# Dual layers: three and a half tiles of the first gate product are multiplied inside the attention loop into a bank of their own; attention outputs use one bank

## The chip, the cores and the metric

One core of a Trainium2 chip runs the whole program in one launch. The metric is device microseconds from the start to the end of an execution. All inputs and outputs are float32.

## The reference, cut to what matters

Two models run one behind the other on 256 tokens of width 1024. The change lies in the second, whose two layers are called "dual" here. Each layer has three branches (a convolution, a neighbourhood attention with 8 heads, a grouped-query attention with 8 query and 2 key heads) and a gate for each branch:

```python
a, naq, nak, nav, gq, gk, gv, gates = split_in(h @ w_in[l])
br_a = conv_branch(a, ...)                                  # layer norm over 512 channels, silu, @ w_conv_out
br_b = na_latent(naq, nak, nav, na_kc, na_vc, na_rpb[l]) @ w_na_out[l]
q = axial_rope(rmsnorm_2(gq, q_norm_g[l]), pos_row, pos_col)
k = axial_rope(rmsnorm_2(gk, k_norm_g[l]), pos_row, pos_col)
br_c = gqa_latent(q, k, gv, g_kc, g_vc) @ w_gqa_out[l]
ga, gb, gc = jnp.split(gates, 3, axis=-1)                   # 3 x 1024 columns of h @ w_in[l]
y = jax.nn.sigmoid(ga) * br_a + jax.nn.sigmoid(gb) * br_b + jax.nn.sigmoid(gc) * br_c
x = x + g1 * (y @ w_out[l])
```

In layer 0 the 256 context tokens go through the same layer beside the 256 latent ones (512 columns, N = 512); in layer 1 only the latent ones do (N = 256), and the context gives keys and values. `g1` and its like come from `silu(c) @ w_mod + b_mod`.

## The kernel before

**Products.** Each weight product is made of three products of rounded parts (`product`, line 698: high by high, high by low, low by high), accumulated in a PSUM bank. A tile of an output is 128 rows by N columns; with an inner dimension of 1024 it has 8 "k steps" of three products each. A "job" is 8 weight tiles of 128 by 128, enough for one output tile of a gate. Weights come as halves of 16 tiles (1 MB) into a ring of four slots, through SP's queue, in the order of STREAM. ACT rounds a job (`round_job`), DVE subtracts to get the low part (`rest_job`, line 1613), and PE waits for that. Four split jobs have room; `ahead(stage, g)` on ACT and on DVE handles the job three behind g. So when the attention loop begins, jobs 0 to 2 of the first gate product are split, and `ahead("gates..", 0)` is the call that splits job 3, `ahead(.., 1)` that of job 4.

**The attention loop** (`softmax`, one version for each of PE, ACT and DVE). A step v takes a pair of heads. PE: the scores of pair v (`score_pair`, banks 4 to 7), at even v the output product of pairs v - 4 and v - 3, then the turns (transposes) of pair v - 2 into banks 2 and 3. DVE: the bias of the neighbourhood heads, the maximum, later the scaling by the inverse sum. ACT: a copy of the turned probabilities, the exponentials, and at odd v, behind the exponentials, the copy of the outputs (`o_free`). Layer 0 has 32 pairs (16 grouped-query, 16 neighbourhood; 2 of each 4 against all 512 keys, 2 against 256), layer 1 has 16. The outputs lie by turns in banks 0 and 1 (`out_banks`), so PE waits for the output copy of two before.

**What follows.** PE waits for the last output copy and multiplies the gate tiles in two groups of four (`gemm_group`, banks 0 to 3). After the fourth and the eighth tile it makes two sums of the convolution's layer norm (`conv_sums`), for which POOL adds the four chunks (`add_chunks`, line 639; `ln_added`); the second of these additions needs ACT's squares of the centred values, which need the first sum. ACT takes the sigmoid of each tile. Then come the 8 tiles of `branch{l}0`, 4 k steps each, and the same for the other two gates.

In layer 0, DVE also has the dot products for the modulation of later layers (`dots`, `mod_half`, line 1634; eight instructions each) behind the splits of tiles 1, 2, 3 and 6, with their weights in the same ring. They need Silu of c: POOL loads c when all outputs are copied (line 633), and ACT takes the Silu behind the sigmoid of tile 0, ahead of everything for tile 1.

Of the kernel before, what the change touches and what calls it, by code (L numbers as in the profile page):

```python
# [45 lines left out]
DH = 64  # L46
# [109 lines left out]
for _name in DOTS_AT:  # L156
# [7 lines left out]


BANKS = [("lru_in", (5,) * 4), ("lru_gate", (0, 0, 0, 0, 3, 3, 2, 2)), ("lru_out", (1,) * 8),
         ("ffn_in0", (12,) * 4), ("ffn_out0", (2,) * 4), ("nsa_q", (2,) * 4), ("nsa_kv", (2,) * 4),
         ("nsa_gate", (0, 0, 1, 0)), ("nsa_v", (1, 1, 0, 0)), ("gate_turned", (0, 0, 0, 1)), ("cmp", (2, 2, 0, 0)),
         ("cmp2", (0, 0, 0, 0, 0, 0, 1, 1)), ("nsa_out", (2,) * 4), ("ffn_in1", (12,) * 4), ("ffn_out1", (2,) * 4)]
for _l in range(DEPTH):  # L170
    BANKS += [(f"conv_in{_l}", (2,) * 4), (f"gq{_l}", (1,) * 4), (f"gkv{_l}", (1, 0, 1, 1)),
              (f"naq{_l}", (1,) * 4), (f"nak{_l}", (1,) * 4), (f"nav{_l}", (1, 1, 0, 0, 0, 0, 1, 1))]
    for _b in range(3):
        BANKS += [(f"gates{_l}{_b}", (2,) * 4), (f"branch{_l}{_b}", (2,) * 4)]
    BANKS += [(f"out{_l}", (2,) * 4), (f"mlp_in{_l}a", (HALF_A,) * 4), (f"mlp_out{_l}a", (2,) * 4),
              (f"mlp_in{_l}b", (HALF_B,) * 4), (f"mlp_out{_l}b", (2,) * 4)]
# [118 lines left out]
def program(nc, wstream, params_in, consts_in, rpb_in, c_in, x_in, out):  # L295
    ctx = ExitStack()
    with ctx:
# [3 lines left out]
        def sem(name):  # L301
            return ctx.enter_context(nc.semaphore(name))
# [123 lines left out]
        cmp_scores = [ps[q][:, 0:HEADS * NCMP] for q in range(2)]  # L426
        nav_banks = (0, 1, 6, 7)

        landed = [sem(f"landed{s}") for s in range(SLOTS)]
# [31 lines left out]
        rotated, centred = sem("rotated"), sem("centred")  # L461
        ln_added = sem("ln_added")
        blocks_ready = sem("blocks_ready")
        branch_rounded, branch_split = sem("branch_rounded"), sem("branch_split")
# [193 lines left out]
        def _(pe):  # L658
# [201 lines left out]

            def softmax(layer=None, begun=0, after={}):

# [3 lines left out]
                for v in range(pairs + 3):  # L866
                    if begun <= v < pairs:
                        score_pair(layer, v)
                    if v >= 4 and v % 2 == 0:

                        i = 2 * (v - 4)
                        kind, t, _, q = jobs[i]
                        out_ = (base + i) // 4
                        if out_ >= 2:
                            pe.wait_ge(o_free, out_ - 1)
                        if layer is None and i == 0:
                            pe.wait_ge(pe_aux_free, 2)
                        if layer is not None and i < 8:
                            pe.wait_ge(acc_free[out_ % 2], USED[f"nav{layer}"][out_ % 2] + 1)
                        pe.wait_ge(turned_ready, (base + i) // 2 + 2)  # L880
# [18 lines left out]
                        for n in range(last + 1):  # L899
                            for p in range(2):  # L900
                                val, pr, first = terms[p][n]
                                ins = mm(out_banks[out_ % 2][DH * p:DH * p + DH, first * P:S], val, pr, start=n == 0, stop=n == last)
                        ins.then_inc(o_full, 1)
# [147 lines left out]
            def dual(l):  # L1051
# [85 lines left out]
                turned_group(f"nav{l}", nav_banks, (f"in{l}", 22), 512, after=in_nav)  # L1137
                softmax(l, begun=2)
                pe.wait_ge(o_free, jobs_done.base // 4)
# [14 lines left out]
                for br in range(3):  # L1154
                    for n in range(2):
                        gemm_group(f"gates{l}{br}", f"gates{l}{br}", n, n, N=N, between=conv_sums(n) if br == 0 else None)
# [29 lines left out]
        def _(act):  # L1186
# [162 lines left out]
            def softmax(layer, after):  # L1349

                jobs = attention_jobs(layer)
                pairs = len(jobs) // 2
                base = jobs_done.base
                for v in range(pairs + 4):
                    if 2 <= v < pairs + 2:
# [6 lines left out]
                        if kind == "nsa" and u == 0:  # L1362
                            act.wait_ge(c_copied, 2)
                        go(used_pair(pT[:, (2 * u) % 4:(2 * u) % 4 + 2, :], kind, q), used_pair(turn_pair, kind, q), ACT.Copy).then_inc(turned_ready, 1)
                    if v < pairs:
                        kind, t, _, q = jobs[2 * v]
                        act.wait_ge(score_max, base // 2 + v + 1)
                        for p in range(2):
# [6 lines left out]
                            ins.then_inc(prob_exp, 1)  # L1375
                    if v >= 5 and v % 2 == 1:
                        n = 2 * (v - 5)
                        kind, t, _, q = jobs[n]
                        out_ = (base + n) // 4
                        act.wait_ge(o_full, out_ + 1)  # L1380
                        o = {"nsa": n_q, "na": a_naq, "gqa": a_gq}[kind]
                        go(o[:, t, q * P:(q + 2) * P], out_banks[out_ % 2][:, 0:S], ACT.Copy).then_inc(o_free, 1)
                    if v in after:
# [54 lines left out]
            def dual(l):  # L1438
# [51 lines left out]

                softmax(l, {1: nav_copies})

                def branch_round(br):

                    if br == 0:
                        act.wait_ge(o_free, jobs_done.base // 4)
                    else:
                        full(f"branch{l}{br - 1}", 3, 1)
# [5 lines left out]
                for br in range(3):  # L1504
                    for n in range(2):
                        for m in range(4):
                            ahead(f"gates{l}{br}", 4 * n + m)
                            copy(f"gates{l}{br}", m, n, a_sig[:, 4 * n + m, 0:N], acc[m][:, 0:N], func=ACT.Sigmoid)
                            if (l, br, n, m) == (0, 0, 0, 0):
# [52 lines left out]
        def _(dve):  # L1562
# [451 lines left out]
            def dual(l):  # L2014
# [103 lines left out]
                dve.wait_ge(conv_done, KC * (l + 1))  # L2118
                softmax(l)

                for br in range(3):
                    st = f"branch{l}{br}"
                    for g in range(8):
                        ahead(f"gates{l}{br}", g)

                        if (br, g) == (0, 4):
                            dve.wait_ge(pe_aux_full, aux.next())
                            link(V.tensor_scalar(rs[:, 0:N], psT[:, 0:N], 1.0 / CW, None, ALU.mult))
                            for c in range(KC):
                                V.tensor_tensor(a_cy[:, c, 0:N], a_cy[:, c, 0:N], rs[:, 0:N], ALU.subtract).then_inc(centred, 1)  # L2130
# [12 lines left out]
                    for m in range(KD + 2 * (br == 2)):  # L2143
# [7 lines left out]
                        if m < 4:  # L2151
                            dve.wait_ge(acc_free[m], USED[f"gates{l}{br}"][m] + 2)
                        o, g, a = a_y[:, m, 0:N], a_sig[:, m, 0:N], acc[m % 4][:, 0:N]
# [222 lines left out]
```

## Time and profile before

| | |
|---|---|
| three runs | 2074.39, 2073.84, 2060.24 us |
| median | 2073.84 us |
| the profiled execution | 2069.44 us, span 2067.6 us |
| mean granted clock of TensorE | 0.982 |
| instructions | 33690 |

Times in rows are microseconds from the span's start. PE is TensorE's products, PEld its weight loads, DVE VectorE, ACT ScalarE, POOL GpSimd. A row of the timeline gives start, duration, engine, line, operation, output<-inputs by name with the shape, the count of merged instructions, and in brackets the idle time ahead with what ended it. Ends of matmuls are modelled, so that neighbouring ones overlap in the rows: the distance from start to start is the cost of one. L666 is a helper that makes all products, L1198 one that makes all ACT operations; their tiles tell which is meant.

### The profile page before, as it was taken

To read this page: it belongs to the slowest core of one execution; us is meant where nothing else is said; L and a number is where in the kernel's file an instruction comes from. 1 tells how busy PE (TensorE), PEld (TensorE's weight loads), DVE (VectorE), ACT (ScalarE), POOL (GpSimd) and SP (SyncE) were. 2 spreads that over 40 slices of the span, in tenths; PEclk is the share of its full clock that TensorE was granted. 3 is DMA by queue.
4 is the path that set the end of the run, shared out by engine and by line. 5 is a ranking of instruction groups with operands and counts; after the bars stand their busy time and mean duration, and the time that the engine had idled before them with its cause. 6 is when DMAs were issued, how large, how long until landed. Compare 5 with 4: busy or idle time off the path is not lost.

```text
span 2067.6 us, 33690 instructions
## 1 busy us (share of the span) xinstructions
PE 1984.2 (96%) x12854; PEld 1748.1 (85%) x12854; DVE 1506.5 (73%) x2738; ACT 897.0 (43%) x1436; POOL 361.4 (17%) x354
## 2 busy tenths in 40 slices
PE   7999999979999999988999999999999998999998
PEld 6999999759999888646888878888888866999998
DVE  7769887697987589776697668575666986675554
ACT  5744445463444432476333332222214456644442
POOL 0013333002325300001100222201231000013223
PEclk9999999999999999999999999999999999999999
DMA  6455575405555422102445225454554311554552
GB/s 259 165 198 190 198 258 191 176 8 218 202 184 207 149 102 83 61 1 97 149 163 194 102 81 201 148 201 184 185 210 164 130 55 42 181 187 164 185 201 82
DMA packets 46990, 318.12 MB, mean 154 GB/s; under 512 B 5008, under 2 KB 8080, under 8 KB 9488
## 3 DMA queue, kind: packets, MB, share of 16 engines
q1 hardware_dynamic: 45568, 309.58, 41.3%
q0 software_dynamic: 1296, 6.82, 1.0%
q8 instruction: 84, 1.38, 0.3%
q14 instruction: 42, 0.34, 0.0%
HBM read 315.33 MB, written 1.05 MB: 153 GB/s over the span
## 4 chain that ended last, share of the span: by engine, by line
PE 86%; DVE 8%; ACT 4%; issue 1%; DMA 0%; POOL 0%; DVEq 0%; ACTq 0%; POOLq 0%
PE ps L666 84%; ACT arena L1198 3%; PE ps L915 2%; DVE arena L2037 2%; DVE small L1843 1%; DVE w_lo L1613 1%; DVE arena L1865 1%; DVE ps L1832 1%; ACT w_hi L1198 1%; DVE arena L1595 0%; ACT L1198 0%; DMA x<-x_in 0%; PE ps L1104 0%; PE ps L1097 0%; DVE rs L1794 0%
## 5 line engine op out<-in xcount | busy, mean ns | idle before, releaser
L666 PE MATMUL ps<-h_hi,w_hi 128*128 128x256 f32 (+2 forms) x2632 | 838.1, 318 | 21.5 <-DVE h_lo L1605 8.2
L666 PE MATMUL ps<-h_lo,w_hi 128*128 128x256 f32 (+2 forms) x2632 | 830.2, 315 | 0.0
L666 PE MATMUL ps<-h_hi,w_lo 128*128 128x256 f32 (+2 forms) x2632 | 829.7, 315 | 0.0
L1613 DVE TENSOR_TENSOR w_lo<-ring,w_hi 128x1024 fp32r<-128x1024 f32 x457 | 583.9, 1284 | 300.0 <-ACT w_hi L1198 299.2
L1198 ACT ACTIVATE w_hi<-ring 128x1024 fp32r<-128x1024 f32 x457 | 479.5, 1055 | 527.3 <-PE ps L666 491.7
L666 PEld LDWEIGHTS ps<-h_hi,w_hi 128*128 128x128 f32 (+1 forms) x2632 | 499.2, 190 | 60.6 <-issue 14.3
L666 PEld LDWEIGHTS ps<-h_lo,w_hi 128*128 128x128 f32 (+1 forms) x2632 | 500.9, 190 | 33.4
L666 PEld LDWEIGHTS ps<-h_hi,w_lo 128*128 128x128 f32 (+1 forms) x2632 | 499.2, 190 | 33.5
L1198 ACT ACTIVATE arena<-ps 128x512 f32<-128x512 f32 (+2 forms) x246 | 140.8, 578 | 343.1 <-PE ps L666 296.3
L666 PE MATMUL ps<-hid_hi,w_hi 128*128 128x256 f32 (+1 forms) x736 | 224.2, 305 | 0.0
L666 PE MATMUL ps<-hid_lo,w_hi 128*128 128x256 f32 (+1 forms) x736 | 224.2, 305 | 0.0
L666 PE MATMUL ps<-hid_hi,w_lo 128*128 128x256 f32 (+1 forms) x736 | 224.1, 305 | 0.0
L1634 DVE SCALAR_TENSOR_TENSOR ps<-ring,arena 128x512 f32<-128x512 f32 x320 | 223.6, 766 | 0.0
L555 POOL CAST hid_hi<-arena 128x256 f32 (+3 forms) x92 | 45.5, 495 | 576.8 <-DVE arena L1778 576.8
L666 PEld LDWEIGHTS ps<-hid_lo,w_hi 128*128 128x128 f32 x736 | 139.0, 189 | 6.8
L666 PEld LDWEIGHTS ps<-hid_hi,w_lo 128*128 128x128 f32 x736 | 138.2, 188 | 6.9
L666 PEld LDWEIGHTS ps<-hid_hi,w_hi 128*128 128x128 f32 x736 | 138.2, 188 | 6.8
L557 POOL TENSOR_TENSOR hid_lo<-arena,hid_hi 128x256 f32 (+3 forms) x92 | 138.8, 1509 | 15.1 <-POOL hid_hi L555 14.4
L666 PE MATMUL ps<-arena 128*64 128x256 f32 (+4 forms) x768 | 124.4, 444 | 17.4 <-ACT arena L1198 15.0
L2037 DVE SCALAR_TENSOR_TENSOR arena<-arena,prm 128x512 f32<-128x512 f32 (+1 forms) x240 | 129.7, 608 | 0.0
L562 POOL TENSOR_TENSOR arena<-x 128x256 f32<-128x256 f32 (+1 forms) x59 | 58.8, 996 | 294.1 <-DVE x L1995 219.0
L666 PEld LDWEIGHTS ps<-arena 128*64 128x64 f32 (+2 forms) x768 | 59.2, 160 | 57.3 <-issue 35.8
(193 smaller groups left out, 1944.4 us busy)
## 6 DMA issues: line engine op xcount, KB each, us to landing
ring<-wstream SPq DMA_DIRECT2D x290, 1024.0 KB, 4.8
arena<-c_in POOLq DMA_DIRECT2D x7, 512.0 KB, 4.1
arena<-rpb POOLq DMA_DIRECT2D x2, 1536.0 KB, 6.5
x<-x_in SPq DMA_DIRECT2D x2, 1024.0 KB, 12.0
out<-arena SPq DMA_DIRECT2D x8, 128.0 KB, 2.0
cst<-consts SPq DMA_DIRECT2D x1, 928.0 KB, 12.0
prm<-params SPq DMA_DIRECT2D x1, 580.0 KB, 10.7
ring<-wstream SPq DMA_DIRECT2D x1, 512.0 KB, 3.8
```

The lines of the kernel that those rows point to most:

```text
L555: nc.gpsimd.tensor_copy(hi, products[:, e, 0:N]).then_inc(pool_step, 1)
L557: nc.gpsimd.tensor_tensor(lo, products[:, e, 0:N], hi.bitcast(F32), ALU.subtract).then_inc(pool_written, 1)
L562: square = nc.gpsimd.tensor_tensor(total if first else one, src, src, ALU.mult)
L666: ins = nc.tensor.matmul(*a, **k)
L915: ins = nc.tensor.transpose(turn_pair[:, p, b * P:(b + 1) * P], s_p[:, (2 * u + p) % 4, b * P:(b + 1) * P], ident)
L1198: return nc.scalar.activation(o, i, f, **k)
L1613: V.tensor_tensor(w_lo[:, job % SPLITS, :], raw_job(job), w_hi[:, job % SPLITS, :].bitcast(F32), ALU.subtract).then_inc(weights_ready, 1)
L1634: V.scalar_tensor_tensor(out=ps[4 + p][:], in0=w, scalar=1.0, in1=c[s][:, p * S2:(p + 1) * S2], op0=ALU.mult, op1=ALU.mult, accum_out=mod_ ...
L1832: ins = V.scalar_tensor_tensor(out=sc, in0=c, scalar=slope, in1=sc, op0=ALU.mult, op1=ALU.add)
L1843: ins = V.tensor_reduce(top, used_pair(score_pairs[v % 2], kind, q), AX, ALU.max, negate=True)
L1865: ins = V.tensor_scalar(o[:, br, :], o[:, br, :], s_rec[:, c:c + 1], None, ALU.mult)
L2037: return V.scalar_tensor_tensor(out=cy[:, c, 0:ns, :], in0=a_u3[:, c, 0:ns, bass.ds(j, S)], scalar=w, in1=cy[:, c, 0:ns, :], op0=ALU.mult, ...
```

## The change

Of the first gate (`gates{l}0`) tiles 0, 1 and 2 and the first four k steps of tile 3 move into PE's attention loop. In layer 0 one k step stands in each of v 3 to 10, 12 to 19 and 21 to 28, and four in v 34, the last; in layer 1 two stand in each of v 3 to 6, 8 to 11 and 13 to 16, and four in v 18, the last. A step stands behind the scores and ahead of the output product. Tiles 0 to 2 go one after another into bank 1. The outputs have bank 0 alone, so that PE waits for the output copy of one before, and ACT makes this copy ahead of the exponentials of the odd v. ACT copies each finished tile to SBUF in the loop (places that are free by then) and takes the three sigmoids from there after the loop. The split of job 3 moves into the loop as well (ACT v 16 and 8, DVE v 18 and 9). The second half of tile 3 stands ahead of the wait for the last output copy; tiles 4 to 7 follow, with the sums after tiles 4 and 7.

```diff
+FILL = 3
+FILL_AT = {0: [(v, 1) for first in (3, 12, 21) for v in range(first, first + KD)] + [(34, 4)],
+           1: [(v, 2) for first in (3, 8, 13) for v in range(first, first + KD // 2)] + [(18, 4)]}
+FILL_DONE = {0: (10, 19, 28), 1: (6, 11, 16)}
+FILL_USES = (1, 4, 1, 2)
+def gate_bank(br, m):
+    if br == 0:
+        return (1, m) if m < FILL else (m % 4, {3: 0, 4: 0, 5: FILL, 6: 0, 7: 1}[m])
+    return m % 4, m // 4
...
+        gate_raw = (rs, part(16640, S2), a_nak[:, 2, :])
+        def out_half(layer, i):
+            return out_banks[i % 2 if layer is None else 0][:, 0:S]
...
+            def gate_steps(l, N):
+                step, at = {}, 0
+                todo = [(m, k) for m in range(FILL + 1) for k in range(KD)]
+                def some(count):
+                    nonlocal at
+                    for m, k in todo[at:at + count]:
+                        b, n = gate_bank(0, m)
+                        if k == 0:
+                            step[m] = job(f"gates{l}0", m)
+                            free(f"gates{l}0", b, n)
+                        ins = product(acc[b][:, 0:N], step[m](k), h_(k, 0, N), k == 0, k == KD - 1)
+                        if k == KD - 1:
+                            ins.then_inc(acc_full[b], 1)
+                            job_done()
+                    at += count
+                return some
...
 # PE, attention loop
                     if begun <= v < pairs:
                         score_pair(layer, v)
+                    if v in amid:
+                        amid[v]()
                     if v >= 4 and v % 2 == 0:
...
-                        if out_ >= 2:
+                        if layer is not None:
+                            pe.wait_ge(o_free, out_)
+                        elif out_ >= 2:
                             pe.wait_ge(o_free, out_ - 1)
...
-                softmax(l, begun=2)
+                gates = gate_steps(l, N)
+                softmax(l, begun=2, amid={v: lambda n=n: gates(n) for v, n in FILL_AT[l]})
+                gates(KD)
                 pe.wait_ge(o_free, jobs_done.base // 4)
...
+                    for m in range(KD if br else FILL + 1, KD):
+                        b, n = gate_bank(br, m)
+                        w = job(f"gates{l}0", m)
+                        free(f"gates{l}0", b, n)
+                        for k in range(KD):
+                            ins = product(acc[b][:, 0:N], w(k), h_(k, 0, N), k == 0, k == KD - 1)
+                        ins.then_inc(acc_full[b], 1)
+                        job_done()
+                        if m in (4, 7):
+                            conv_sums(m // 7)(3)
...
 # ACT
-                softmax(l, {1: nav_copies})
+                def gate_copy(m):
+                    copy(f"gates{l}0", 1, m, gate_raw[m][:, 0:N], acc[1][:, 0:N])
+                softmax(l, {1: nav_copies, 16 // (l + 1): lambda: ahead(f"gates{l}0", 0), **{v + l: lambda m=m: gate_copy(m) for m, v in enumerate(FILL_DONE[l])}})
...
-                            ahead(f"gates{l}{br}", 4 * n + m)
-                            copy(f"gates{l}{br}", m, n, a_sig[:, 4 * n + m, 0:N], acc[m][:, 0:N], func=ACT.Sigmoid)
+                            if br + n + m:
+                                ahead(f"gates{l}{br}", 4 * n + m)
+                            if br + n + m == 0:
+                                act.wait_ge(acc_free[1], USED[f"gates{l}0"][1] + FILL)
+                                for f in (2, 0, 1):
+                                    ins = go(a_sig[:, f, 0:N], gate_raw[f][:, 0:N], ACT.Sigmoid)
+                                ins.then_inc(raw_squashed, 1)
+                            elif br or n or m >= FILL:
+                                b, turn = gate_bank(br, 4 * n + m)
+                                copy(f"gates{l}{br}", b, turn, a_sig[:, 4 * n + m, 0:N], acc[b][:, 0:N], func=ACT.Sigmoid)
                             if (l, br, n, m) == (0, 0, 0, 0):
                                 act.wait_ge(c_landed, 96)
...
 # DVE
-                softmax(l)
+                softmax(l, after={18 // (l + 1): lambda: ahead(f"gates{l}0", 0)})
```

## Rows read from the trace of the kernel before

**Rows 1.** The page's first part: busy time and share of the span.
```profile
PE 1984.2 (96%) x12854; PEld 1748.1 (85%) x12854; DVE 1506.5 (73%) x2738; ACT 897.0 (43%) x1436; POOL 361.4 (17%) x354
```

**Rows 2.** Windows of one loop period each: us, then busy time by engine, clock.
```profile
885.01:895.97 10.96, 9.69 (x68) 5.51 (x64) 7.77 (x20) 8.94 (x24) 0.00 (x0) 1.00 0.01 1
919.58:930.86 11.28, 9.75 (x64) 5.50 (x64) 8.66 (x20) 8.29 (x24) 0.00 (x0) 1.00 0.00 0
1699.16:1705.82 6.66, 6.15 (x40) 3.37 (x40) 4.77 (x11) 5.25 (x12) 0.00 (x0) 1.00 0.00 0
1705.82:1712.30 6.48, 6.15 (x40) 3.38 (x40) 5.28 (x12) 5.07 (x12) 0.00 (x0) 1.00 0.00 0
```

**Rows 3.** Timeline of layer 0's loop: waits of PE, the last at its end.
```profile
919.70 1.72 PE L666 MATMUL ps<-arena 64*128 64x256 f32 x12 [0.38 <-ACT arena L1198]
...
924.15 1.06 PE L915 MATMUL ps<-cst,arena 128*128 128x128 f32 x8 [0.57 <-ACT arena L1198]
...
953.70 1.08 PE L666 MATMUL ps<-arena 128*64 128x256 f32 x8 [0.78 <-ACT arena L1198]
```

**Rows 4.** Timeline of PE, gate products: first and last of 18, then of 19.
```profile
995.72 0.39 PE L666 MATMUL ps<-h_hi,w_hi 128*128 128x512 f32 x1
...
999.57 0.40 PE L666 MATMUL ps<-h_hi,w_lo 128*128 128x512 f32 x1
...
1763.83 0.28 PE L666 MATMUL ps<-h_hi,w_lo 128*128 128x256 f32 x1
...
1765.87 0.28 PE L666 MATMUL ps<-h_hi,w_lo 128*128 128x256 f32 x1
```

**Rows 5.** Timeline by engine from the end of layer 0's loop to the branch's end.
```profile
954.82 0.38 ACT L1198 ACTIVATE arena<-ps 128x256 f32<-128x256 f32 x1 [0.99 <-PE ps L666]
956.17 1.28 ACT L1198 ACT_TABLE_LOAD   x1
961.03 0.60 ACT L1198 ACTIVATE arena<-ps 128x512 f32<-128x512 f32 x1 [3.58 <-PE ps L666]
962.94 2.01 ACT L1198 ACTIVATE arena<-arena 128x1024 f32<-128x1024 f32 x2
964.85 1.04 ACT L1198 ACTIVATE w_hi<-ring 128x1024 fp32r<-128x1024 f32 x1
...
965.92 1.23 DVE L1613 TENSOR_TENSOR w_lo<-ring,w_hi 128x1024 fp32r<-128x1024 f32 x1 [6.96 <-ACT w_hi L1198]
...
955.50 1.04 POOL L633 DMA_DIRECT2D arena<-c_in  x2 [259.12 <-ACT arena L1198]
...
992.30 5.77 POOL L639 TENSOR_TENSOR arena<-arena 128x512 f32<-128x512 f32 x3 [30.82 <-ACT arena L1198]
...
999.80 1.03 PE L666 MATMUL ps<-arena,ones 128*128 128x256 f32 x4
1000.48 0.58 PE L666 MATMUL ps<-branch_hi,w_hi 128*128 128x512 f32 x1
...
1022.66 0.39 PE L666 MATMUL ps<-h_hi,w_hi 128*128 128x512 f32 x1
```

**Rows 6.** DMA issues of the same stretch: KB each, us to landing.
```profile
arena<-c_in POOLq DMA_DIRECT2D x2, 512.0 KB, 4.3
```

**Rows 7.** Windows around an idle stretch of PE: columns as in rows 2.
```profile
699.00:704.00 5.00, 2.73 (x10) 2.37 (x11) 2.80 (x9) 1.69 (x4) 0.00 (x0) 0.50 0.49 204
704.00:708.00 4.00, 4.00 (x11) 3.13 (x10) 4.00 (x10) 3.42 (x7) 0.00 (x0) 0.50 0.00 0
708.00:712.00 4.00, 4.00 (x18) 3.27 (x18) 4.00 (x10) 0.96 (x2) 0.00 (x0) 0.97 0.50 170
```

**Rows 8.** Timeline of layer 1: the loop's last output product, and what follows.
```profile
1739.22 3.54 PE L666 MATMUL ps<-arena 128*64 128x256 f32 x16 [1.21 <-ACT arena L1198]
...
1746.36 0.38 ACT L1198 ACTIVATE arena<-ps 128x256 f32<-128x256 f32 x1 [0.93 <-PE ps L666]
...
1759.77 3.24 POOL L639 TENSOR_TENSOR arena<-arena 128x256 f32<-128x256 f32 x3 [13.27 <-ACT arena L1198]
...
1765.99 0.61 PE L666 MATMUL ps<-arena,ones 128*128 128x128 f32 x4
```

More of the change, by code:

```diff
@@ L173 @@
     for _b in range(3):
-        BANKS += [(f"gates{_l}{_b}", (2,) * 4), (f"branch{_l}{_b}", (2,) * 4)]
+        BANKS += [(f"gates{_l}{_b}", (2,) * 4 if _b else FILL_USES), (f"branch{_l}{_b}", (2,) * 4)]
     BANKS += [(f"out{_l}", (2,) * 4), (f"mlp_in{_l}a", (HALF_A,) * 4), (f"mlp_out{_l}a", (2,) * 4),
@@ L462, in program @@
         ln_added = sem("ln_added")
+        raw_squashed = sem("raw_squashed")
         blocks_ready = sem("blocks_ready")
@@ L859, in score_pair, with softmax @@
                 ins.then_inc(score_full, 1)
-            def softmax(layer=None, begun=0, after={}):
+            def gate_steps(l, N):
[14 more added lines that the diff above has]
+                return some
+            def softmax(layer=None, begun=0, after={}, amid={}):
                 jobs = attention_jobs(layer)
@@ L877, in softmax @@
                             pe.wait_ge(pe_aux_free, 2)
-                        if layer is not None and i < 8:
-                            pe.wait_ge(acc_free[out_ % 2], USED[f"nav{layer}"][out_ % 2] + 1)
+                        if layer is not None and i == 0:
+                            pe.wait_ge(acc_free[0], USED[f"nav{layer}"][0] + 1)
                         pe.wait_ge(turned_ready, (base + i) // 2 + 2)
@@ L901, in softmax @@
                                 val, pr, first = terms[p][n]
-                                ins = mm(out_banks[out_ % 2][DH * p:DH * p + DH, first * P:S], val, pr, start=n == 0, stop=n == last)
+                                ins = mm(out_half(layer, out_)[DH * p:DH * p + DH, first * P:S], val, pr, start=n == 0, stop=n == last)
                         ins.then_inc(o_full, 1)
@@ L1154, in dual @@
                 for br in range(3):
-                    for n in range(2):
-                        gemm_group(f"gates{l}{br}", f"gates{l}{br}", n, n, N=N, between=conv_sums(n) if br == 0 else None)
+                    for n in range(2 if br else 0):
+                        gemm_group(f"gates{l}{br}", f"gates{l}{br}", n, n, N=N)
+                    for m in range(KD if br else FILL + 1, KD):
[8 more added lines that the diff above has]
+                            conv_sums(m // 7)(3)
                     for m in range(KD):
@@ L1353, in softmax, with attention_out @@
                 base = jobs_done.base
+                def attention_out(v):
+                    if v >= 5 and v % 2 == 1:
+                        n = 2 * (v - 5)
+                        kind, t, _, q = jobs[n]
+                        out_ = (base + n) // 4
+                        act.wait_ge(o_full, out_ + 1)
+                        o = {"nsa": n_q, "na": a_naq, "gqa": a_gq}[kind]
+                        go(o[:, t, q * P:(q + 2) * P], out_half(layer, out_), ACT.Copy).then_inc(o_free, 1)
                 for v in range(pairs + 4):
@@ L1364, in softmax @@
                         go(used_pair(pT[:, (2 * u) % 4:(2 * u) % 4 + 2, :], kind, q), used_pair(turn_pair, kind, q), ACT.Copy).then_inc(turned_ready, 1)
+                    if layer is not None:
+                        attention_out(v)
                     if v < pairs:
@@ L1375, in softmax @@
                             ins.then_inc(prob_exp, 1)
[L1376 to L1382, printed above, removed]
+                    if layer is None:
+                        attention_out(v)
                     if v in after:
@@ L1496, in branch_round @@
                         act.wait_ge(o_free, jobs_done.base // 4)
+                        act.wait_ge(raw_squashed, l + 1)
                     else:
@@ L2123, in dual @@
                     for g in range(8):
-                        ahead(f"gates{l}{br}", g)
+                        if br + g:
+                            ahead(f"gates{l}{br}", g)
                         if (br, g) == (0, 4):
                             dve.wait_ge(pe_aux_full, aux.next())
+                            dve.wait_ge(acc_free[3], USED[f"gates{l}0"][3] + 1)
                             link(V.tensor_scalar(rs[:, 0:N], psT[:, 0:N], 1.0 / CW, None, ALU.mult))
@@ L2151, in dual @@
                         if m < 4:
-                            dve.wait_ge(acc_free[m], USED[f"gates{l}{br}"][m] + 2)
+                            dve.wait_ge(acc_free[m], USED[f"gates{l}{br}"][m] + (2 if br else FILL_USES[m]))
                         o, g, a = a_y[:, m, 0:N], a_sig[:, m, 0:N], acc[m % 4][:, 0:N]
```

## The prediction

> **What bounds the kernel now.** I read the page first. TensorE (PE) is busy 96% of the span [rows 1], so a change that only moves products can gain no more than PE's idle time in the stretches that it touches. I looked for that next, with the busy time in windows cut at the loop's own period. In layer 0 four pairs of heads (two against 512 keys, two against 256) make a period: PE works 9.69 of 10.96 us in the grouped-query half and 9.75 of 11.28 us in the neighbourhood half, so it idles 1.27 and 1.53 us; in layer 1 two pairs make one, with 0.51 and 0.33 us idle [rows 2]. The timeline says where: each idle piece is one wait of PE on ScalarE (ACT) or VectorE (DVE), 0.4 to 0.6 us long, ahead of a score or a turn, and 0.78 us at the loop's end [rows 3]. ACT works 8.94 of 10.96 us there and DVE 7.77. The loop is a ring of three engines, with PE nearly its bound.
>
> Then I followed what starts when the loop ends in layer 0, engine by engine [rows 5]. PE goes straight on with the gate product. But another chain begins there too: the last output is copied (end at 955.2, called T0), POOL issues the load of c (955.50), ACT takes the Silu of c (962.94), rounds the next weights (964.85), DVE splits them (965.92) and works without a gap through the dot products of the modulation, which its program has between the splits; after them come the centring, the squares, POOL's additions (992.30 to 998.07) and at last the two sums on PE (999.80). In the kernel before this chain is hidden by a hair: PE reaches the second sums 1.7 us after POOL has them ready.
>
> **The change, part by part.** *Fill.* A k step of the first gate product is three products: 18 products of 512 columns start in 3.85 us (17 intervals), 0.2265 us each, so a step is 0.68 us; in layer 1, with 256 columns, 19 rows span 2.04 us, 0.113 us each, and two steps again make 0.68 us [rows 4]. 28 steps move into each layer's loop: 19.0 us of PE in layer 0, 9.5 us in layer 1. The work is the same, so the time changes only by idle time that goes or comes.
>
> *Layer 0, in the loop.* 24 single steps lie in v 3 to 28, six periods' worth. Each period gets four steps, 2.72 us, against 1.27 or 1.53 us idle, so PE becomes the bound and at most 3 x 1.27 + 3 x 1.53 = 8.4 us are absorbed [rows 2]. Are all the idle pieces reached? The 0.57 us ahead of a turn follows a score, and the step is put between; the 0.38 us ahead of a score waits for ACT's exponentials of two pairs before, and PE is now later by a step too [rows 3]. Yes, but ACT gets three copies of a finished tile (0.60 us each) and one rounding (1.05 us), DVE one split (1.23 us) inside the ring [rows 5]: together 4.1 us, with PE no longer waiting most of it is slack; I count 1.4 us. Absorbed: 7.0 us; the bounds are 8.4 and, if every step sits on the ring's latency, 0. The single bank for outputs costs nothing: an output bank is written every second v, and its 0.38 us copy is now made before the exponentials of the odd v. That copy and the moved order are covered by PE's longer round; without the cover it is 0.38 us in each of 8 periods, 3 us. The four steps at v 34 (2.72 us) stand ahead of the last output product, which waited 0.78 us [rows 3]. So the last copy, T0, is later by 19.0 - 7.0 - 0.8 = 11.2 us.
>
> *Layer 0, after the loop.* PE has only half a tile left and then tile 4. Its weights are split by the `ahead(1)` of ACT and DVE, and on ACT that stands behind the three sigmoids and the Silu of c. ACT needs 1.28 (table) + 3 x 0.60 + 1.28 = 4.4 us after T0; c lands about 0.3 + 0.5 + 4.3 = 5.2 us after T0 (issue at 955.50, the second load 0.5 later, 4.3 us each) [rows 5, 6]. The load waits for all outputs as before, so c decides: Silu at T0 + 5.2, where it was at 962.94, T0 + 7.7. The chain is therefore 2.5 us earlier against T0, and no more, while PE reaches tile 4 at T0 + 2.3. PE will wait for tile 4 until 5.2 + 2.0 (two Silu) + 1.05 + 1.23 = T0 + 9.5, and again for tiles 6 and 7 and at the second sums. From the Silu to POOL's last addition is 998.07 - 962.94 = 35.1 us of DVE, ACT and POOL, which the change leaves alone; then 0.7 us of sums and 1022.66 - 1000.48 = 22.2 us of the branch product. Before, the branch ended at T0 + 67.5; now at T0 + 5.2 + 35.1 + 0.7 + 22.2 = 63.2. Only 4.3 us of the 19.0 come back. Layer 0 so far: 11.2 - 4.3 = +6.9 us.
>
> *The clock in layer 0.* The granted clock was 1.00 nearly everywhere; where PE idled 2.3 of 5 us it was 0.50 (1.2 GHz), and in the following 4 us of full work still 0.50 and back at 0.97 in the next 4 [rows 7]: some 6 us of work at half speed, 3 us lost. PE's first new wait (T0 + 2.3 to 9.5) costs nothing so, since the chain is later anyway. The last one, from the end of tile 7 (about T0 + 36) to the sums at T0 + 40.3, is 4 us, with the branch product right behind: +3 us. Layer 0: +9.9 us. The Trainium skill (TensorE: Matmul & The Clock Gate, Part 1) says that the default state is throttled and that activity releases the throttle; the trace agrees (0.50 behind the idle stretch). By that rule alone the steps in the loop could also save: they could keep the clock up.
>
> *Layer 1.* Six times two v have steps, against 0.51 or 0.33 us idle (mean 0.42, 2.5 us), v 16 a little more, 2.8 us, less 0.7 us for the copies and the split: 2.1 us [rows 2]. The four steps at v 18 (1.36 us) fill a wait of 1.21 us. The output product behind it took 3.54 us for 16 products, at half clock, where 8 take 1.08 us in layer 0 [rows 3, 8]; with three waits of 1.2 us filled in part I expect full clock: 1.4 us saved. T0 of this layer is later by 9.5 - 2.1 - 1.2 - 1.4 = 4.8 us. Behind it there is no c: `ahead(1)` is through at 1.28 + 3 x 0.38 + 1.05 + 1.23 = 4.7 us, and PE, done with tile 3 at about 0.9, waits 3.8 us. Then four tiles of 2.72 us and 1.0 us of sums end at 16.6, where they ended at 22.8 before (from 1739.2 + 3.5 + a copy of 0.4 to 1765.99): 6.2 back, net -1.4 us. POOL's additions (to 1763.0) move forward with the first sums and stay just hidden [rows 8]. The wait of 3.8 us can pull the clock down like the one above, with nothing to hide it: +2.8. Layer 1: +1.4 us.
>
> *Sum.* 9.9 + 1.4 = +11.3 us on the profiled execution's 2069.4 us (its span 2067.6): 2080.7. The median of the runs shown is 2073.8, 4.4 us above the profiled one, within their spread of 14 us; I let the sum stand at 2081.
>
> **Rivals.** *The clock stays up* in both new waits: less 3.0 and 2.8, 2075. For it: the falls depend on where in time a wait lies; against it: the row above. *The steps don't fit the ring*: each lengthens it by its whole 0.68 us, because PE's burst, the turned copy and the exponentials follow one another in a closed chain at each even v. Then the 7.0 and 2.1 us aren't absorbed: 2090; from about 12 us of lost cover it is over 1%. For it: the chain of layer 1 runs through the burst. Against: at odd v there is slack. *Other side, faster*: what follows the loop is bound by PE alone and never by the split weights, so all idle time absorbed stays a gain: 8.4 + 0.8 + 2.8 + 1.2 + 1.4 = 14.6, 2055. It decides if tile 4's weights come before PE does, within 2.3 us of T0. Against it speaks the order of ACT's program; for it, that PE never waited there before. The Trainium skill (Perfetto Trace Analysis, Identifying the Most-Contended Engine) holds matmul busy time to be a bad measure of headroom and wants the weight loads' instead. The loads are busy 5.51 of 10.96 us [rows 2], which by that rule leaves room for all four steps and makes this rival's time 2055 the forecast. I hold to the starts in the timeline: inside the burst one product follows the other.
>
> **How the numbers follow.** Forecast 0.45; clock stays up 0.22; steps don't fit 0.18; faster 0.15. The range leaves out most of the last and the far end of the third: 2061 to 2094. A change of 1%, 21 us, is about what can be told from none. Faster by that needs 2053 or less, beyond even the rival's sum: 0.05. Slower needs 2095, the third rival with its 3 us of copies and a longer first wait: 0.11. Within: 0.84.
>
> **What would show it.** In the profile after: layer 0's loop longer by about 11 us, with PE over 97% busy in v 3 to 28; a PE wait on split weights of about 7 us right after it, further waits of about 4 us in all of tiles 6 and 7 and about 4 us ahead of the second sums; the branch product ending some 7 to 10 us later than before; in layer 1 a wait of 3.8 us and a loop longer by 5. I am wrong if the Silu of c starts much earlier or later than 5 us after the last copy, if DVE's dot products are shorter than now, or if PE's loads of weights between float kinds cost time that the trace before doesn't show.

## The result and the profile after

The changed kernel takes 2084.44 us (median of 8 runs, 2079.74 to 2089.32), the kernel before beside it 2073.32 us (8 runs, 2060.24 to 2075.24): the ratio is 1.0075, with an interval of 1.0054 to 1.0096. By the ratio it is 15.6 us slower, the two medians lie 11.1 us apart, and the forecast was +11.3. The time is inside the range, and the change is under the 1% that the prediction took as the least to be told from none. The profiled execution took 2087.44 us, with a span of 2085.6 us.

The page's head, with the busy time of the engines that [rows 1] shows for before:

```profile
span 2085.6 us, 33731 instructions
PE 1995.7 (96%) x12854; PEld 1753.3 (84%) x12854; DVE 1503.4 (72%) x2738; ACT 899.4 (43%) x1442; POOL 362.5 (17%) x354
```

PE has the same 12854 products and is busy 11.5 us longer, and the span is 18.0 us longer: something in the products themselves has become dearer, and new waits have come. To see where, I cut both profiled executions at the same instructions, by their starts in the timeline: PE's first turn in the loop, POOL's first addition behind it (in before and after it starts 1.4 us behind T0 in layer 0, and 0.1 us behind it in layer 1 of after), and DVE's last product for the sum y of the first branch. The forecasts behind the loops are the prediction's terms with its clock terms added (-4.3 + 3.0 and -6.2 + 2.8).

| us | before | after | difference | forecast |
|---|---|---|---|---|
| layer 0, loop | 92.8 | 104.0 | +11.2 | +11.2 |
| layer 0, loop's end to branch's end | 66.3 | 64.7 | -1.6 | -1.3 |
| layer 1, loop | 54.5 | 65.3 | +10.8 | +4.8 |
| layer 1, loop's end to branch's end | 34.3 | 29.2 | -5.1 | -3.4 |
| the two layers | | | +15.3 | +11.3 |

The other 2.7 of the span's 18.0 us lie in stretches that the change doesn't touch: 1.7 us before the first loop, a piece that alone varies from 856.1 to 866.6 us over the runs below.

**Layer 0's loop.** Windows of one period each (us, then busy time by engine, granted clock, DMA share), where [rows 2] has 10.96 and 11.28 us:

```profile
895.93:908.71 12.78, 12.78 (x78) 7.40 (x78) 8.05 (x22) 9.28 (x23) 0.00 (x0) 1.00 0.00 0
908.71:921.40 12.69, 12.69 (x76) 7.32 (x76) 9.90 (x22) 9.31 (x23) 0.00 (x0) 1.00 0.01 2
933.75:946.53 12.78, 12.78 (x79) 7.39 (x78) 8.71 (x21) 8.29 (x22) 0.00 (x0) 1.00 0.00 1
1704.39:1712.08 7.69, 7.69 (x54) 4.90 (x54) 4.88 (x11) 5.09 (x10) 0.00 (x0) 1.00 0.00 0
```

PE is busy for the whole of each period, in layer 1 (last line) too; the waits of [rows 3] are gone where steps stand. Two stay at v 11 and 20, which have no step, 0.57 and 0.33 us, and so do those at the loop's end. The loads (second pair) are busy 7.4 of 12.78 us.

**Behind layer 0's loop.** The waits of PE from 965 to 1035 us (engine, line, releaser: us in total, times, longest):

```profile
PE ps L686 <- issue: 7.2, 1, 7.2
PE ps L686 <- POOL arena L659: 3.9, 1, 3.9
PE ps L686 <- DVE w_lo L1690: 1.4, 1, 1.4
```

"issue" means that the profile names no releaser. That this wait is for tile 4's split weights I read from the times: DVE's split ends at 977.77, PE starts at 977.87.

And the timeline of the chain that [rows 5] shows for before:

```profile
967.73 0.38 ACT L1254 ACTIVATE arena<-ps 128x256 f32<-128x256 f32 x1 [2.88 <-PE ps L686]
968.41 1.05 POOL L653 DMA_DIRECT2D arena<-c_in  x2 [270.23 <-ACT arena L1254]
...
973.56 2.00 ACT L1254 ACTIVATE arena<-arena 128x1024 f32<-128x1024 f32 x2 [1.16 <-DMA arena<-c_in]
975.47 1.04 ACT L1254 ACTIVATE w_hi<-ring 128x1024 fp32r<-128x1024 f32 x1
976.54 1.23 DVE L1690 TENSOR_TENSOR w_lo<-ring,w_hi 128x1024 fp32r<-128x1024 f32 x1 [14.84 <-ACT w_hi L1254]
977.87 0.76 PE L686 MATMUL ps<-h_hi,w_hi 128*128 128x512 f32 x1 [7.20 <-issue]
...
1002.92 5.71 POOL L659 TENSOR_TENSOR arena<-arena 128x512 f32<-128x512 f32 x3 [29.45 <-ACT arena L1254]
...
1008.68 1.65 PE L686 MATMUL ps<-arena,ones 128*128 128x256 f32 x3 [3.85 <-POOL arena L659]
```

With T0 at 968.1 the Silu stands at T0 + 5.4 and waits for c; tile 4 starts at T0 + 9.8 behind a wait of 7.2 us; POOL's additions end at T0 + 40.5, and the sums had waited 3.85 us for them.

### The profile page after: what moved, and what is told of

Read it like the earlier page. It is cut to its first block, busy times and chain, and to the rows that moved or that the text cites. A ratio compares the mean times of both kernels' runs of the same rounds, so it can differ in the third digit from the quotient of the medians.

```text
span 2085.6 us, 33731 instructions
## 1 busy us (share of the span) xinstructions
PE 1995.7 (96%) x12854; PEld 1753.3 (84%) x12854; DVE 1503.4 (72%) x2738; ACT 899.4 (43%) x1442; POOL 362.5 (17%) x354
## 4 chain that ended last, share of the span: by engine, by line
PE 87%; DVE 8%; ACT 3%; issue 1%; DMA 1%; POOL 0%; DVEq 0%; ACTq 0%
PE ps L686 84%; ACT arena L1254 2%; PE ps L959 2%; DVE arena L2114 2%; DVE w_lo L1690 1%; DVE small L1920 1%; DVE arena L1942 1%; DVE ps L1711 1%; ACT w_hi L1254 1%; DVE ps L1909 1%; DVE arena L1672 0%; DMA x<-x_in 0%; PE ps L1148 0%; POOL arena L659 0%; ACT L1254 0%
## 5 line engine op out<-in xcount | busy, mean ns | idle before, releaser
L1254 ACT ACTIVATE arena<-ps 128x256 f32<-128x256 f32 (+2 forms) x244 | 137.5, 580 | 348.0 <-PE ps L686 280.3
L1254 ACT ACTIVATE arena<-ps,small 128x512 f32<-128x512 f32 (+2 forms) x162 | 90.1, 569 | 19.2 <-PE ps L686 8.5
## 6 DMA issues: line engine op xcount, KB each, us to landing
prm<-params SPq DMA_DIRECT2D x1, 580.0 KB, 10.8
```

The source lines that it names most:

```text
L1254: return nc.scalar.activation(o, i, f, **k)
```

## The experiments

The same cuts for every kernel below, in us (start: up to layer 0's first turn; mid: between the layers' stretches; rest: behind layer 1's first branch):

| | start | L0 loop | L0 behind | mid | L1 loop | L1 behind | rest |
|---|---|---|---|---|---|---|---|
| before | 863.8 | 92.8 | 66.3 | 665.9 | 54.5 | 34.3 | 290.1 |
| after | 865.5 | 104.0 | 64.7 | 666.3 | 65.3 | 29.2 | 290.6 |
| e1_layer0_only | 866.1 | 104.0 | 63.9 | 669.7 | 52.9 | 33.9 | 291.3 |
| e2_layer1_only | 858.5 | 91.0 | 66.3 | 669.5 | 63.7 | 29.2 | 290.4 |
| e3_copy_early | 856.1 | 102.4 | 63.9 | 668.2 | 59.9 | 29.1 | 290.3 |
| e4_split_first | 863.5 | 104.0 | 62.4 | 667.4 | 63.7 | 29.2 | 289.8 |
| e5_dots_moved | 857.8 | 104.1 | 56.3 | 667.2 | 65.3 | 29.1 | 296.6 |
| e6_three | 856.4 | 104.0 | 48.3 | 667.4 | 59.9 | 27.9 | 300.3 |
| e7_before_dots_moved | 858.5 | 91.1 | 66.3 | 667.8 | 54.3 | 33.9 | 290.2 |
| e8_after_again | 857.9 | 104.0 | 63.9 | 669.0 | 63.7 | 29.2 | 290.9 |
| e9_pairs | 865.6 | 107.6 | 64.0 | 666.5 | 65.3 | 29.4 | 289.9 |
| e10_three_pairs | 866.6 | 107.6 | 48.3 | 665.4 | 59.9 | 27.5 | 290.1 |

Where two kernels have the same program in one of the four stretches, it repeats to 0.4 us, or differs by 0.8 or by 1.4 to 1.8 us; start, mid and rest differ by some 10 us whatever the kernel. So a mechanism is read from its own stretch, and the timed comparison decides only over some 5 us.

### Each layer's part alone

e1 has the change in layer 0 alone, e2 in layer 1 alone; the other layer runs as before:

```diff
+FILLED = (0,)   # e2: (1,)
...
-                gates = gate_steps(l, N)
-                softmax(l, begun=2, amid={v: lambda n=n: gates(n) for v, n in FILL_AT[l]})
-                gates(KD)
+                if l in FILLED:
+                    gates = gate_steps(l, N)
+                    softmax(l, begun=2, amid={v: lambda n=n: gates(n) for v, n in FILL_AT[l]})
+                    gates(KD)
+                else:
+                    softmax(l, begun=2)
```

> The change is made in layer 0 alone; layer 1 is as before. By the prediction's chain (what follows the loop of layer 0 hangs on the load of c, the Silu, the dot products, the centring and POOL's additions) it is 10 us slower than before (9 to 12), and layer 1 keeps its old span, 1684 to 1743 shifted. By the rival that the steps don't fit the ring, layer 0's loop alone is longer by 19 us and the whole is 15 or more slower. If most of the loss were in layer 1, this kernel would be within 3 us of before.

> The change is made in layer 1 alone. The prediction had +1.4 us here. The trace after shows two waits that it did not have: PE waits 1.95 and 1.76 us for ACT's copy of the finished tile out of bank 1 before the next tile may begin, and a fall of the clock behind the first. By that, 5 to 7 us slower than before. If these waits were covered by others, +1 to +2.

Beside 2066.49 us for the kernel before (18 runs), e1 took 2080.24 (6 runs; 1.0066, 1.0040 to 1.0092) and e2 2076.50 (10 runs; 1.0049, 1.0025 to 1.0072). By the cuts e1 loses 11.2 us in layer 0's loop and gets 2.4 back, e2 loses 9.2 in layer 1's and gets 5.1 back. Each layer costs, and layer 1 costs several times the forecast 1.4 us. Layer 1, untouched in e1, has its last output product at 1.95 us and not at the 3.54 of [rows 8], with the same three waits of 1.2 us ahead, and its loop takes 52.9 us: the slow product belongs to the execution and not to these waits alone.

### A copy that stands one step too late

The cut of layer 1's loop named a term that I hadn't sized, so I read PE's rows there. After, from the timeline of PE:

```profile
1719.57 1.13 PE L686 MATMUL ps<-arena 64*128 64x512 f32 x4 [0.36 <-ACT arena L1254]
1722.64 0.36 PE L686 MATMUL ps<-h_hi,w_hi 128*128 128x256 f32 x1 [1.95 <-ACT rs L1254]
...
1745.83 0.36 PE L686 MATMUL ps<-h_hi,w_hi 128*128 128x256 f32 x1 [1.76 <-ACT arena L1254]
```

Both are the first product of a new tile, at v 8 and v 13. PE can't write bank 1 before ACT has copied the tile in it, and in layer 1 the copy stands at v 7 and 12, one v behind the last step, where ACT comes to it behind the exponentials of scores which PE has only just made. In layer 0 the copy is at v 10 and the next tile begins at v 12: no such wait. Behind the first wait the clock fell, too: in the window 1719.80 to 1727.50 it was 0.78, and of eight output products of 16, all of 1.95 us but this one, one took 3.60:

```profile
1719.80:1727.50 7.70, 5.75 (x30) 2.95 (x29) 3.77 (x8) 2.70 (x7) 0.00 (x0) 0.78 0.01 2
```

The fall doesn't come in every execution with this wait: the same output product took 3.60, 3.44 and 3.51 us in after, e5 and e9, and 1.95 us in e2, e4 and e8.

e3 makes the copy in the v of the tile's last step:

```diff
-                softmax(l, {1: nav_copies, 16 // (l + 1): ..., **{v + l: lambda m=m: gate_copy(m) for m, v in enumerate(FILL_DONE[l])}})
+                softmax(l, {1: nav_copies, 16 // (l + 1): ..., **{v: lambda m=m: gate_copy(m) for m, v in enumerate(FILL_DONE[l])}})
```

> The changed kernel, with ACT's copies of the finished tiles in layer 1 one v earlier (v 6, 11 and 16 in place of 7, 12 and 17), so that the bank is free when the next tile begins. If the two waits and the clock's fall behind them are the missed part: both waits gone, 3.7 us, and 1.6 us of clock, so 5 us faster than the changed kernel (2079). If the ring takes the time elsewhere, less than 2 us.

It took 2077.57 us (7 runs) beside 2066.49: 1.0061, 1.0031 to 1.0091. Waits of PE in layer 1's loop, e3 first, then after:

```profile
PE ps L959 <- ACT arena L1254: 1.9, 2, 1.2
PE ps L686 <- ACT arena L1254: 1.4, 3, 0.7
```

```profile
PE ps L686 <- ACT arena L1254: 3.1, 4, 1.8
PE ps L686 <- ACT rs L1254: 1.9, 1, 1.9
PE ps L959 <- ACT arena L1254: 1.9, 2, 1.2
```

Both waits are gone, 3.7 us, and the slow product with them: 3.60 - 1.95 = 1.65 us. Together that is 5.4 us, and the loop went from 65.3 to 59.9. Where the waits came without the fall (e2, e4, e8) the loop takes 63.7, so the copy's place costs 3.8 us without the fall and 5.4 with it. This term is shown. The timed runs agree in sign but can't tell 5 us.

### What PE waits for behind layer 0's loop

In the forecast tile 4 waits for its split weights, and DVE's chain through c sets the branch's end anyway. If the wait for the weights were itself the loss, splitting them earlier would get it back. e4 rounds and splits the two next jobs ahead of the sigmoids, in layer 0 (ACT):

```diff
-                            if br + n + m:
+                            if br or 4 * n + m > 2 or (m and l not in (0,)):
                                 ahead(f"gates{l}{br}", 4 * n + m)
                             if br + n + m == 0:
+                                for g in range(1, 3 if l in (0,) else 1):
+                                    ahead(f"gates{l}0", g)
```

> The changed kernel, with ACT's roundings of jobs 4 and 5 in layer 0 ahead of the sigmoids and of the Silu of c. It takes away what PE waited 7.2 us for. By the prediction's chain that gives next to nothing: PE begins tile 4 about 7 us earlier but the second sums still wait for POOL, 0 to 2 us faster than the changed kernel, with the wait ahead of the sums longer instead. If the wait on the split weights were itself the loss, it is 7 us faster (2077) or more.

The waits of PE behind the loop, e4, from the timeline:

```profile
969.99 0.47 PE L686 MATMUL ps<-h_hi,w_hi 128*128 128x512 f32 x1 [1.30 <-issue]
...
980.81 0.62 PE L686 MATMUL ps<-h_hi,w_hi 128*128 128x512 f32 x1 [4.22 <-DVE w_lo L1692]
...
995.79 0.50 PE L686 MATMUL ps<-h_hi,w_hi 128*128 128x512 f32 x1 [2.24 <-DVE w_lo L1692]
...
1005.38 2.07 PE L686 MATMUL ps<-arena,ones 128*128 128x256 f32 x4 [3.85 <-POOL arena L659]
```

The 7.2 us at tile 4 shrank to 1.3 and came back as 4.2 and 2.2 at later tiles, since DVE's program has eight dot products, which need c, between the splits of jobs 4 and 5; the wait for POOL is the same 3.85 us. The stretch is 62.4 us where it was 64.7 and 63.9: at most 2.3 us of 7. The chain through c and DVE sets the end. The timed median (2090.05, 4 runs; 1.0134, 1.0104 to 1.0164) lies above the changed kernel's and above e4's own profiled execution (span 2079.9); nothing in its rows accounts for it, and I leave it open.

e5 takes eight dot products from behind each of tiles 1, 2 and 3 of the first gate and has them behind tile 5 of all three gates; the number of dot products stays 12 times eight:

```diff
-"gates00": (1, 2, 3, 6), "gates01": (1, 2, 3, 6), "gates02": (1, 2, 3, 6),
+"gates00": (5, 6), "gates01": (1, 2, 3, 5, 6), "gates02": (1, 2, 3, 5, 6),
...
-                        if (l, br, g) == (0, 0, 1):
+                        if (l, br, g) == (0, 0, 5):
                             dve.wait_ge(c_ready, 6)
```

e7 is the same edit of the kernel before, as a control.

> The changed kernel, with the dot products of the modulation behind the loop of layer 0 put elsewhere: of the four beside the first gate product two (at 5 and 6, so behind the centring) stay, the other two go to the second and the third gate. The split order on ACT, and with it the wait of 7.2 us for tile 4, is left alone. If DVE's dot products are what the second sums wait for, POOL's second additions begin about 10 us sooner after the loop and the stretch from the loop's end to the end of the branch product falls from 64.7 to about 57 us, 7 us in all. If the load of c and the splits alone set the end, it stays within 2 us.

> The kernel before with the dot products moved as in e5, the control for e5 and e6. There PE is the bound behind the loop, so nothing should change: the same time as before within 2 us, and 66 us from the loop's end to the branch's end. If the dot products already cost time before, it is faster, and e6's gain is theirs.

POOL's loads of c and its two additions, e5:

```profile
960.83 1.04 POOL L653 DMA_DIRECT2D arena<-c_in  x2 [269.47 <-ACT arena L1254]
961.89 3.98 POOL L659 TENSOR_TENSOR arena<-arena 128x512 f32<-128x512 f32 x3
982.98 5.22 POOL L659 TENSOR_TENSOR arena<-arena 128x512 f32<-128x512 f32 x3 [17.11 <-ACT arena L1254]
```

The second addition starts 21.1 us after the first, where it was 33.4; PE's only wait left is the first:

```profile
970.21 0.77 PE L686 MATMUL ps<-h_hi,w_hi 128*128 128x512 f32 x1 [7.12 <-issue]
```

The stretch is 56.3 us, 8.4 less than after and 7.6 less than the 63.9 of its repeats. Before, the same edit leaves it at 66.3 and the time at 2065.48 (10 runs; 0.9999, 0.9981 to 1.0018): there PE was the bound, "by a hair", as the prediction read from [rows 5]. e5 took 2075.28 us (10 runs) beside 2065.85 (25 runs): 1.0047, 1.0026 to 1.0068. The changed kernel once more, beside the same runs of before, e8:

> The changed kernel once more, on the chip of these runs: 15 us slower than before, as first measured, 104 and 64.7 us in layer 0's loop and behind it, 64 to 65 and 29 in layer 1's.

It took 2086.45 (4 runs; 1.0105, 1.0075 to 1.0135), so 15 to 28 us slower, where the first comparison gave 11 to 20.

### Three causes removed

e6 has e3's copies, e4's order in both layers, and e5's dot products.

> The changed kernel with all three edits at once: the tile copies of layer 1 one v earlier, jobs 4 and 5 rounded first in both layers, and the dot products moved as in e5. If the prediction's chain and the two waits of layer 1 are the whole loss, little is left to wait for: from the loop's end to the branch's end 49 us in layer 0 (64.7 in the changed kernel) and 25 in layer 1 (29.2), its loop 60 (65.3); together 25 us less than the changed kernel, 2060, so 10 to 14 us faster than before. If the loops' lengthening is a loss that the products after them can't return, it ends at before's time or above.

e6 took 2058.90 us (10 runs) beside 2065.85: 0.9974, 0.9950 to 0.9999. The stretch behind layer 0's loop fell from 64.7 to 48.3 us, that of layer 1 to 27.9, layer 1's loop to 59.9. It is 27.6 us faster than e8 beside it. Beside the kernel before it is faster by so little that the interval nearly reaches 1; its four stretches agree, 240.1 us in all where before has 247.9 and e7, whose dot products stand as here, 245.6. With most waits gone, a part of the absorbed idle time stays a gain.

### The price of a step in the loop

A step costs more inside the loop than its three products. Timeline of PE, after:

```profile
944.68 0.50 PE L686 MATMUL ps<-h_hi,w_hi 128*128 128x512 f32 x1
...
945.50 1.03 PE L959 MATMUL ps<-cst,arena 128*128 128x128 f32 x8
...
947.52 0.50 PE L686 MATMUL ps<-h_hi,w_hi 128*128 128x512 f32 x1
...
948.41 1.95 PE L686 MATMUL ps<-arena 128*64 128x256 f32 x16
```

Rows of the two other products of each step are left out. From a step's start to the next work it is 0.82 us ahead of turns and 0.89 us ahead of an output product, not 0.68. PE goes there from the float32 products of the attention to the rounded kind (fp32r) and back. The shape of the products changes at the same places, and no run here separates the two. e9 halves the number of these changes by steps in twos:

```diff
-FILL_AT = {0: [(v, 1) for first in (3, 12, 21) for v in range(first, first + KD)] + [(34, 4)],
+FILL_AT = {0: [(v, 2) for first in (3, 12, 21) for v in range(first, first + KD, 2)] + [(34, 4)],
```

> Layer 0's steps stand in twos at every second v (3, 5, 7, 9, then 12, 14, 16, 18, then 21, 23, 25, 27) where they stood singly; everything else is as in the changed kernel. The theory tested: a step costs 0.82 to 0.90 us inside the loop where its three products are 0.68, because PE changes between the float kinds of the steps and of the attention's products on both sides. PE was busy for the whole of each period, so twelve changes fewer, at 0.15 to 0.20 us, shorten layer 0's loop from 104.0 to about 102 us; in layer 1, where steps stand in twos, nothing changes. The rival: the 0.15 us are not a cost of the change of kind, or the larger bursts of 1.4 us hold up the ring; then the loop keeps 104.0 us or becomes longer by some us, with waits of PE on ACT or DVE in its rows. In the timed comparison 2 us cannot be told from none; the verdict is the length of the loop in the profiled execution.

The loop became longer, 107.6 us, and e9 took 2088.24 us (7 runs) beside 2066.95: 1.0090, 1.0055 to 1.0125. Windows of one period, e9:

```profile
925.70:938.86 13.16, 12.50 (x77) 7.53 (x77) 8.71 (x21) 8.76 (x24) 0.00 (x0) 1.00 0.12 49
938.86:952.03 13.17, 12.52 (x76) 7.55 (x76) 8.71 (x21) 8.28 (x23) 0.00 (x0) 1.00 0.01 2
```

And its PE in one period, with the two waits:

```profile
938.86 1.95 PE L686 MATMUL ps<-arena 128*64 128x256 f32 x16 [0.33 <-ACT arena L1254]
...
942.38 0.50 PE L686 MATMUL ps<-h_hi,w_hi 128*128 128x512 f32 x1
...
943.88 0.60 PE L959 MATMUL ps<-cst,arena 128*128 128x128 f32 x4
...
945.44 1.08 PE L686 MATMUL ps<-arena 128*64 128x256 f32 x8 [0.33 <-ACT arena L1254]
```

From the output product at v 6 to the one at v 28, after first, then e9:

```profile
878.77:948.41 69.64, 68.74 (x413) 39.76 (x412) 46.91 (x113) 49.75 (x127) 0.00 (x0) 1.00 0.05 16
879.06:952.03 72.97, 68.01 (x412) 40.26 (x412) 46.69 (x112) 49.62 (x125) 0.00 (x0) 1.00 0.05 15
```

The rival was right about the length, the theory in part about the price. In the periods shown PE's busy time fell from 12.78 to 12.5 us for two bursts fewer, 0.14 us each, the size that the starts show ahead of turns (2 x 0.82 - 1.50, the two steps here). But bursts of two make PE wait 0.33 us for ACT ahead of each output product: 0.66 us come for 0.28 saved. Where the twos stand at even v (12 to 18), ahead of output products, a period is as long as 13.93 us, with waits of 0.56 and 0.57, and its busy time is 12.80 us beside 12.77: nothing saved there. Over the whole stretch ten bursts fewer save 0.7 us of busy time, and PE's idle time grows from 0.9 to 5.0 us. So what a burst costs hangs on where it stands, and that the change of float kind is the cause is not shown. The closed chain of the rival "the steps don't fit the ring" holds for steps in twos; single steps stay just inside it.

> The three edits of e6 (early copies, splits ahead of the sigmoids, dot products moved away from the first gate's splits) and the steps in twos in layer 0. Expected beside the kernel before: faster by 7 us as e6 (0.997), and by some 2 us more if the changes of float kind cost what their rows show, so 2064 where before is 2073. Layer 0's loop 102 us, its tail 48.3; layer 1's loop 59.9, its tail 27.9. By the rival of e9 the loop of layer 0 stays at 104 us or above and the whole equals e6.

e10 took 2068.41 us (12 runs) beside 2066.95 (20 runs): 1.0005, 0.9981 to 1.0029. Its layer 0 loop is 107.6 us, 3.6 more than e6's, its other stretches are e6's to 0.4 us. By the stretches e6 is the faster of the two; the intervals of their timed ratios overlap.

## Why the prediction was right, and where it was mis-sized

**Layer 0, in the loop.** Forecast +11.2, measured +11.2, in part by luck. The absorbed idle time was sized right: PE's waits behind the loop's first turn sum to 12.3 us before and 4.5 after, so 7.8 us went, where the forecast had 7.0 + 0.8. But I let the steps cost their 0.68 us each, and a step costs more inside the loop, which the prediction's last sentence names as a risk. A period shows 12.78 - 9.69 - 2.72 = 0.37 us more for its four steps, 0.31 in the second half. That is 0.08 to 0.09 us a step, beside 0.07 to 0.14 us a burst in e9. The missed term is hidden in +11.2 because the profiled execution of before had a lower clock in the first 9 us of its loop; before, e7 (whose loop has the same program) and after:

```profile
863.75:872.75 9.00, 8.43 (x40) 4.72 (x40) 3.98 (x11) 5.06 (x12) 0.00 (x0) 0.62 0.00 0
858.52:867.52 9.00, 8.71 (x48) 5.17 (x48) 3.98 (x11) 6.01 (x14) 0.00 (x0) 0.81 0.00 0
865.45:874.45 9.00, 9.00 (x48) 5.71 (x49) 3.98 (x11) 5.07 (x12) 0.00 (x0) 0.81 0.00 0
```

0.19 x 9 = 1.7 us, and indeed this loop takes 91.0 and 91.1 us in e2 and e7, where before has 92.8. At the same clock the loop is 13.0 us longer, 1.8 more than forecast. In e3, with 1.00 in these 9 us, the changed loop takes 102.4.

**Layer 0, after the loop.** Right step by step: Silu at T0 + 5.4 (forecast 5.2), the wait at tile 4 7.2 us (7.2), POOL's end T0 + 40.5 (40.3), the wait ahead of the sums 3.85 (4). I had further waits of tiles 6 and 7 at 4 us in all; they are 1.4, because tiles that begin late anyway don't wait again, which moves nothing, since the chain decides. e4 and e5 show that it decides: feeding PE sooner gives 2.3 us at most, shortening DVE's chain gives 7.6 to 8.4. The clock fell behind the last wait as forecast; the window right behind it and the next:

```profile
1008.00:1012.00 4.00, 3.32 (x8) 2.67 (x9) 4.00 (x11) 1.06 (x1) 0.62 (x1) 0.50 0.00 0
1012.00:1016.00 4.00, 4.00 (x16) 3.19 (x15) 3.55 (x8) 0.00 (x0) 0.00 (x0) 0.79 0.25 68
```

That is 3.3 us and then 4 us at 0.50 and 0.79, 0.5 x 3.3 + 0.21 x 4 = 2.5 us lost (3.0 forecast).

**Layer 1, in the loop.** This is the step that failed: +4.8 forecast, +10.8 measured. The sentence "less 0.7 us for the copies and the split" took a copy for its 0.38 us on ACT. What it cost was PE's wait for it, 1.95 and 1.76 us, and in this execution the fall of the clock behind the first, 1.65 us: 5.4 us by e3. I had looked at whose buffer comes free when for the outputs, and not for the gates' own single bank. Without that term the sum is 5.4 us for this loop, 0.6 from the forecast. The 1.4 us that I counted as saved, because the filled waits would keep the clock up, did come (3.54 to 1.95 us), but e1 has 1.95 us with the waits unfilled: that saving is the execution's and is not shown to be the change's. With no fall on either side the loop went from 52.9 (e1) to 63.7 us (e2).

**Layer 1, after the loop.** Forecast 3.4 us back, measured 5.1. The wait is 3.5 us (3.8 forecast), and the clock fell as forecast, but less; the windows behind the wait:

```profile
1766.90:1770.40 3.50, 0.03 (x1) 0.06 (x1) 1.23 (x1) 3.49 (x10) 1.16 (x2) 1.00 0.00 0
1770.40:1774.00 3.60, 3.60 (x21) 3.60 (x22) 2.79 (x4) 2.94 (x4) 0.00 (x0) 0.64 0.20 27
1774.00:1778.00 4.00, 4.00 (x34) 4.00 (x34) 3.82 (x9) 1.50 (x5) 0.00 (x0) 0.90 0.80 266
```

0.36 x 3.6 + 0.10 x 4.0 = 1.7 us, not 2.8.

**The rivals.** The clock does not stay up. The steps fit the ring one at a time, and not in twos (e9). The other side, faster, failed where the prediction said it would be decided: tile 4's weights weren't there within 2.3 us of T0. When the experiments put them there but for 1.3 us and took DVE's chain away (e6), the kernel became faster than before, by 7 us in the medians and not the rival's 14.6: the dearer steps keep a part of the rest, and so do a wait of 1.3 us ahead of tile 4 in layer 0, one of 1.7 us there in layer 1, and one of 1.5 us for POOL ahead of layer 1's second sums (e6, at 1751.78). The Trainium skill (Perfetto Trace Analysis, Identifying the Most-Contended Engine) judges TensorE's headroom by MFU and the loads' busy share. By the loads' share the four steps would have cost the loop nothing; with them the loads are busy 7.4 of 12.78 us, PE has no gap, and the loop is 11 to 13 us longer. Here the rows decide against it.

## What to carry to other kernels

Work moved into a loop's gaps gains only what the stretch it left can give back: look first for the chain that starts when the loop ends, and shorten that, or the gap reappears there. For each buffer that the moved work writes, find the instruction that frees it and what stands ahead of it on its own engine; a copy of 0.4 us one step late cost 3.8 us, and 5.4 where the clock fell. Here steps did better one at a time than in twos, and each cost more inside the loop than among its like. Compare stretches with those of a second execution of the same program before calling a forecast met: a clock dip of 1.7 us hid a missed term here.

## What the runs showed of the hardware

In the last stretch the same 1488 products took one of two times, with a granted clock of 1.00 in both; from the chains of before and e6:

```profile
1888.82 168.94 PE ps L666 x1488
```

```profile
1879.19 175.54 PE ps L686 x1488
```

The windows 1915 to 1935 us hold 179 products in before and 172 in e6:

```profile
1915.00:1935.00 20.00, 20.00 (x179) 20.00 (x178) 11.37 (x12) 8.25 (x10) 7.63 (x8) 1.00 0.58 208
```

```profile
1915.00:1935.00 20.00, 20.00 (x172) 20.00 (x171) 10.05 (x11) 8.50 (x11) 6.43 (x7) 1.00 0.51 165
```

Ten of the twelve profiled executions had the shorter time and two (e5 and e6) the longer. e7 with e5's dot products and e10 with e6's edits have the shorter, which speaks for the execution and against the edit as its cause; no kernel was profiled in both. The pitch, 0.1135 or 0.118 us, is no matter of the granted clock, and its cause stays open; 6.6 us of difference between two profiled executions can come from it alone, more than some of the mechanisms studied here.
